# Low parts of weights all on VectorE, and GpSimd's convolution sums behind them, in a fused two-block transformer layer on one Trainium2 core

## The reference

```python
h = rms_norm(x, norm1_g[l])
z = h @ w_in[l].astype(h.dtype)
glu_in, q, k, v, gate_logits = jnp.split(z, SPLITS, axis=-1)
a_val, a_gate = jnp.split(glu_in, 2, axis=-1)
a = a_val * jax.nn.sigmoid(a_gate)
a = causal_depthwise_conv(a, conv_w[l], conv_b[l])      # 31 taps
a = jax.nn.silu(rms_norm(a, conv_norm_g[l]))
y_a = a @ w_conv_out[l].astype(a.dtype)
# q, k normed by head; attention in three dilated windows -> o
y_b = o @ w_attn_out[l].astype(o.dtype)
x = x + (g_a * y_a + g_b * y_b) @ w_out[l].astype(x.dtype)
```

## Time and profile before

| | before |
|---|---|
| median of 3 runs | 888.81 us |
| the profiled execution | 888.88 us, span 886.9 us |
| TensorE busy | 846.8 us, 95% |
| VectorE busy | 656.4 us, 74%, 1118 instructions |
| ScalarE busy | 555.2 us, 63% |
| GpSimd busy | 293.8 us, 33%, 292 instructions |
| low parts on VectorE (L1332) | 251, mean 1297 ns |
| low parts on GpSimd (L1863) | 16, mean 2592 ns |
| sums on GpSimd (L1912) | 90, mean 968 ns |
| granted TensorE clock, mean | 0.991 |

### The profile page before, as it was taken

How to read it: one execution, slowest core, us unless ns; L and a number is a source line. 1 busy time by engine, 2 the same in 40 slices (tenths; PEclk the granted TensorE clock), 3 DMA queues, 4 the chain that set the end, 5 groups by cost and what they waited for, 6 DMA issues and landing times.

```text
span 886.9 us, 16521 instructions
## 1 busy us (share of the span) xinstructions
PE 846.8 (95%) x5984; PEld 792.0 (89%) x5984; DVE 656.4 (74%) x1118; ACT 555.2 (63%) x1009; POOL 293.8 (33%) x292
## 2 busy tenths in 40 slices
PE   4999969999999999999999999999999999999996
PEld 3998969999998899999888988999997888888885
DVE  5988898897688889777676758747578866666552
ACT  5676976887655677666455675556645765555441
POOL 3799973445523234333121210001022332222111
PEclk9999999999999999999999999999999999999998
DMA  5564454444465547566565435335445466565641
GB/s 204 197 206 176 159 161 125 144 143 142 145 176 181 167 125 218 182 189 182 180 215 190 162 110 177 119 120 166 120 143 160 149 205 188 193 189 176 215 141 48
DMA packets 42304, 146.11 MB, mean 165 GB/s; under 512 B 4704, under 2 KB 7024, under 8 KB 42224
## 3 DMA queue, kind: packets, MB, share of 16 engines
q1 hardware_dynamic: 41472, 143.67, 50.8%
q10 hardware_dynamic: 752, 1.39, 0.4%
HBM read 144.00 MB, written 1.05 MB: 164 GB/s over the span
## 4 chain that ended last, share of the span: by engine, by line
PE 82%; DVE 8%; ACT 3%; issue 3%; POOL 1%; DMA 1%; DVEq 0%; ACTq 0%; POOLq 0%
PE px L516 20%; PE px L520 14%; PE px L522 14%; PE px L521 14%; PE px L517 10%; DVE wlo L1332 2%; PE px L562 2%; PE px L526 1%; PE px L528 1%; PE px L527 1%; DVE px L1391 1%; PE px L584 1%; PE px L719 1%; DVE sq L1347 1%; DVE hx L1353 1%
## 5 line engine op out<-in xcount | busy, mean ns | idle before, releaser
L1332 DVE TENSOR_TENSOR wlo<-raw,whi 128x1024 fp32r<-128x1024 f32 x251 | 323.9, 1297 | 32.9 <-ACT whi L858 32.7
L520 PE MATMUL px<-hx,whi 128*128 128x256 f32 x1072 | 312.3, 291 | 8.2 <-DVE hx L1353 5.0
L858 ACT ACTIVATE whi<-raw 128x1024 fp32r<-128x1024 f32 x267 | 279.9, 1052 | 57.3 <-PE px L517 28.0
L521 PE MATMUL px<-hx,whi 128*128 128x256 f32 x1072 | 304.6, 284 | 0.0
L522 PE MATMUL px<-hx,wlo 128*128 128x256 f32 x1072 | 304.5, 284 | 0.0
L520 PEld LDWEIGHTS px<-hx,whi 128*128 128x128 f32 x1072 | 206.8, 193 | 13.1 <-DVE hx L1353 6.1
L521 PEld LDWEIGHTS px<-hx,whi 128*128 128x128 f32 x1072 | 207.1, 193 | 0.4
L522 PEld LDWEIGHTS px<-hx,wlo 128*128 128x128 f32 x1072 | 206.8, 193 | 0.0
L516 PE MATMUL px<-fx,whi 128*128 128x512 f32 x330 | 115.7, 393 | 0.0
L516 PE MATMUL px<-hx,whi 128*128 128x512 f32 x320 | 111.3, 392 | 1.1 <-DVE hx L1353 1.1
L1912 POOL TENSOR_TENSOR CA<-CA,ct 128x256 f32<-128x256 f32 x90 | 87.1, 968 | 64.3 <-ACT ct L925 55.7
(11 more groups left out here) (300 smaller groups left out, 1363.5 us busy)
## 6 DMA issues: line engine op xcount, KB each, us to landing
raw<-ws SPq DMA_DIRECT2D x267, 512.0 KB, 3.7
tb<-tabs SPq DMA_DIRECT2D x16, 128.0 KB, 2.6
out<-X SPq DMA_DIRECT2D x4, 256.0 KB, 2.5
X<-xs SPq DMA_DIRECT2D x1, 512.0 KB, 4.7
X<-xs ACTq DMA_DIRECT2D x1, 512.0 KB, 4.8
vc<-vecs ACTq DMA_DIRECT2D x1, 320.0 KB, 6.6
msk<-lmask ACTq DMA_DIRECT2D x1, 256.0 KB, 2.9
ug<-pos ACTq DMA_DIRECT2D x1, 128.0 KB, 3.9
```

The costliest lines, as they stand in the source:

```text
L520: e.matmul(b[:, 0:S], H, xh, start=first, stop=False)
L521: e.matmul(b[:, 0:S], H, xl, start=False, stop=False)
L858: e.activation(whi[:, n % NSL, :], raw[:, n % NRAW, :], ACT.Copy).then_inc(s_hi, 1)
L1332: e.tensor_tensor(wlo[:, n % NSL, :], raw[:, n % NRAW, :], whi[:, n % NSL, :], ALU.subtract).then_inc(s_lov, 1)
```

## The change

All 267 low parts are now VectorE's; GpSimd's sixteen are gone, with their semaphore. GpSimd's sums of a chunk wait, up to chunk 56, until VectorE has made the low part that belongs to that step (`LOW[ahead(c)]`). The quotas of taps are new: VectorE 2.9 up to chunk 23, 2.6 up to 33, then 3.5; ScalarE/GpSimd 2.0 up to 33, then 1.8. The last taps now stand at chunk 52 instead of 55. Nothing of the computation changes.

```diff
@@ conv_plan
     for c in range(CONV_END + 1):
-        quota = (2.9, 2.0 if c < 24 else 1.7)
+        quota = (2.9 if c < 24 else 2.6 if c < 34 else 3.5, 2.0 if c < 34 else 1.8)
@@ semaphores
-        def on_gpsimd(c):
-            return c < 64 and c % 4 == 3
-
-        LOW = {}
-        for c in range(n_chunks):
-            n = c // 4 if c < 64 else 16
-            LOW[c] = (s_log, c // 4 + 1) if on_gpsimd(c) else (s_lov, c + 1 - n)
+        LOW = {c: (s_lo, c + 1) for c in range(n_chunks)}
@@ VectorE, lows
                     made[0] += 1
-                    if on_gpsimd(n):
-                        continue
                     e.wait_ge(s_hi, n + 1)
@@ GpSimd (lows and beside are removed, and every call of them)
             def taps(c):
+                if c in TAPS_G and c <= CONV_END:
+                    e.wait_ge(*LOW[ahead(c)])
                 for i, j in TAPS_G.get(c, ()):
@@ GpSimd, the loop over q, k and gate jobs
                 w, i = QKG[m]
-                beside((w, i))
                 taps(first_chunk((w, i)))
                 conv_square(first_chunk((w, i)))
```

More of the change, by code:

```diff
@@ L388, in two_blocks @@
         s_tb = [sem(f"s_tb{i}") for i in range(3)]
-        s_hi, s_lov, s_log, s_mm = sem("s_hi"), sem("s_lov"), sem("s_log"), sem("s_mm")
+        s_hi, s_lo, s_mm = sem("s_hi"), sem("s_lo"), sem("s_mm")
         s_bank = [sem(f"s_bank{i}") for i in range(8)]
@@ L1332, in lows @@
                     e.tensor_tensor(wlo[:, n % NSL, :], raw[:, n % NRAW, :], whi[:, n % NSL, :], ALU.subtract).then_inc(
-                        s_lov, 1)
+                        s_lo, 1)
             def beside(key):
@@ L1850, in _ @@
         def _(e):
[L1851 to L1868, removed]
             def low_tiles(inst, to, behind=None):
@@ L1923, in _ @@
                 for key in (("ag", i), ("av", i)):
-                    beside(key)
                     taps(first_chunk(key))
@@ L1928, in _ @@
                 for c in range(first_chunk(("v", n)), last_chunk(("v", n)) + 1):
-                    lows(ahead(c))
                     taps(c)
@@ L1940, in _ @@
                 qkg(m)
-            beside(("ao", 0))
             taps(CONV_END)
@@ L1947, in _ @@
             for i in range(1, KD):
-                beside(("ao", i))
                 for n in SILUS.get(i, ()):
```

## The result

The changed kernel takes 881.20 us (median of 5 runs, 881.03 to 883.95) against 888.81 us (887.64 to 890.41): a ratio of 0.9916, with an interval of 0.9896 to 0.9936. The forecast was 879.3 us and its range 877.0 to 885.5. The profiled execution took 881.09 us, for a span of 879.3.

What follows compares the result with a forecast made beforehand. TensorE's queue was taken to set the end, its one large wait being 7.3 us at the second scores for a late VectorE. Gains 8.1 - 0.6 + 0.6 + 1.5 = 9.6 us; 888.9 - 9.6 = 879.3 us, range 877.0 to 885.5.

Steps and rivals of the forecast that it cites:

- the forecast's own branch: The main outcome: a stop of 0 to 2.0 us at the second scores, 877.5 to 881 us, chance 0.74.
- one wait is several times all the others: TensorE's waits: 7.3 us once at the scores for VectorE, against 1.5 before w_conv_out and 0.6 at the start.
- start, GpSimd's low part of chunk 3: TensorE's small wait at the start: VectorE, idle there, can make this low part first; gain 0.6 us (0 to 0.6).
- second scores, stop and clock: At the second scores, VectorE frees TensorE's PSUM bank earlier: 9.05 less a remaining stop of 0.9, gain 8.1 us.
- attention steps: From 140 to 220 us: VectorE's load same or lower, but eight taps in chunks 38 and 39; 0.6 us lost.
- wait before w_conv_out: TensorE's 1.5 us stop for the last gated halves on VectorE goes; gain 1.5 us (0 to 1.5).
- I let it start there again: VectorE's stretch before the first softmax was assumed to start at 91.89 us as before, chunk 27's low part filling idle time.
- (a): Rival: blocked time partly moves, 0.62 us per step; 4.0 us stop at second scores, half clock, 884.1 us; chance 0.13.
- A low part rarely meets a sum any more: Before the first softmax, the added wait largely keeps GpSimd's sums off VectorE's low parts; 3.7 us blocked by sums taken.
- VectorE gets 1.14 for it and loses 2.7: Before w_conv_out: VectorE takes over one low part (1.14 us), and its gating falls from 3.81 to 1.1 us.
- (b): Rival: no relief, VectorE's 11.6 us of blocked time stay and only the small gains remain; 888.9 us; chance 0.05.
- (c): Rival: slower, the added wait releases both GpSimd sums against VectorE, 1.48 us blocked per step; 899 us; chance 0.08.

## Why the prediction was right, and the step that was not

The mechanism held. GpSimd's low parts blocked VectorE's K, Q and low parts; without them the first softmax comes early enough for TensorE to stop for 2 us instead of 7, and the clock stays up behind that stop. But the forecast's own branch was missed by a little: its range was 877.5 to 881 and its stop 0 to 2.0 us, against 881.2 and 2.13. Of its signs, the clock of 1.00 up to 250 us and the absence of a wait near 27 us came; low parts at 1.2 us did not (1.55), and four were missed narrowly: Q and K under 0.9 us (1.02), the softmax by 127 (127.48), scores less than 2.1 us behind the head sums (2.13), under 0.5 us before w_conv_out (0.52). Also, "one wait is several times all the others" holds only among the waits that the change can touch. The longest wait of TensorE is at the start, before and after:

```profile
PE px L541 <- DVE sqa L1369: 9.6, 1, 9.6
```

```profile
PE px L535 <- DVE sqa L1361: 9.9, 1, 9.9
```

Term by term, as gains:

| term | predicted | measured |
|---|---|---|
| start, GpSimd's low part of chunk 3 | 0.6 | 0.69 |
| second scores, stop and clock | 8.1 | 6.83 |
| attention steps | -0.6 | -0.58 |
| wait before w_conv_out | 1.5 | 0.97 |
| behind w_conv_out | 0 | -0.3 |
| sum, in the span | 9.6 | 7.6 |

**The start.** Right in place and size: 0.69 us by the head sums, and 1.00 in the second profile of the changed kernel, by the first scores (118.76 before, 117.76). Moving the tiles of chunks 3 and 63 alone removed it too.

**The second scores: the mis-sized term.** I took a stop of 0.9 us; it is 2.13. VectorE ended the softmax at 127.48 instead of the 127.0 forecast, and TensorE was there for the bank at 125.49 instead of 126.1, since the 0.69 us from the start had brought it forward. I had added the start's gain to the sum, though ahead of a stop that VectorE ends it only makes the stop longer. So to the third scores I had promised 8.7 us in all, and 7.52 came; of the 2.0 us by which the sum is too high, 1.2 lie here, 0.5 before w_conv_out and 0.3 behind it.

The end at 127.0 was nearly right by luck: two errors cancel. "I let it start there again" was wrong: the low part of chunk 28, which had started at 91.89, starts at 89.60, 2.3 us earlier, because ScalarE no longer waits for GpSimd's sums. I had read the releaser of that idle time (ScalarE's high part) and not what held ScalarE. And the blocked time is not 3.7 us. From 89.60 to 127.48 are 37.9 us; less 31.4 of own work and 0.3 of waiting, 6.2 us are blocked. By steps from 91.89 on, 3.4 of it falls on ten low parts (14.8 us for 10 x 1.14) and 2.4 on Q and K. That is 0.56 us per step, nearer to the 0.62 of rival (a) than to the 0.34 that I took. "A low part rarely meets a sum any more" fell: that was to be the work of the added wait, and the kernel without the wait has the same low parts (1525 and 1554 ns).

**The added wait.** I had put its cost at nothing, and no cost shows; but no gain shows either, and I had let it save part of the blocked time. What is saved goes by who comes first at chunk 24's step.

**The quotas.** I booked them as two taps less and as 0.6 us lost at the sixth scores. The second is what the runs show (a stop of 1.03 us there, of which 0.3 us are won back by the eleventh; with VectorE's quota old there is none). What I never priced is GpSimd's part, a quota of 2.0 for 1.7 from chunk 24 on. It makes the 2.13 us stop: without it there is none at the second scores. Its price is 3.3 us at w_conv_out between the variants with VectorE's quota old (241.03 against 237.76), of which some 1.5 is that profile's half clock.

**Before w_conv_out.** "VectorE gets 1.14 for it and loses 2.7" is what happened (the gating at L1458 takes 1.08 us for three instructions at 235.02), but TensorE still waits 0.52 us. I took the upper end of 0 to 1.5; measured 0.97.

**The rivals.** (a), 884.1, had the mechanism of the error right, blocked time that partly moves: 6.2 us. It needed 6.8 from 91.89 on, and a half clock, which came in three variants with nearly the same stop and not in this kernel. (b) is out. (c) needed 0.9 us blocked per step; over eleven steps there are 0.56. The rule that spoke against the change (the Trainium skill, Perfetto Trace Analysis, section Optimizing Scalar/DVE Operations: a saturated VectorE may hand work to GpSimd, unless the shared port spoils it) is settled by the run with the low parts alone: with the 16 tiles on GpSimd w_conv_out comes 11.6 us later. Its second half is the one that holds here.

**What stays open.** That the order of arrival at one step decides the next thirty microseconds is shown for its trigger, by one profile of one variant (one sum less in the step of chunk 24); what it is worth in time is not clear of the spread. How the state keeps itself up was read from the two groups of means, not tested: VectorE and GpSimd both take their pace from ScalarE's high parts and products, so an offset between them could persist. Why stops of 2.0 to 2.3 us brought a half clock in three of the kernels and none in the others was not settled. Nor was it settled why the part behind w_conv_out takes 635.1 us in one profile and 639.3 in another that has the same half clock.

## What to carry to other kernels

An instruction's duration in a profile may be mostly someone else's: look for the same form at its shortest, and for what the other engine runs beside its longest. When work moves between VectorE and GpSimd, price the blocked time on both, and follow what starts a stretch back more than one engine, since GpSimd's backlog came round through ScalarE as a late start on VectorE. And take a change with several parts apart: here one part was worth 11.6 us at w_conv_out and the parts added to help it gave 3.7 back.

## What the runs showed of the hardware

A VectorE instruction with two sources in SBUF and a GpSimd instruction that reads two tensors there hold each other up, in both directions. A Q of 0.48 us took 2.54 beside a GpSimd subtraction of 2.60, and GpSimd's sums went from 823 to 1218 ns where VectorE's low parts came first. VectorE's taps, with one source in PSUM, kept 0.48 us. Two memsets of 128 x 1024 (1.96 us) did not block the low part beside them. One small GpSimd instruction less, in one step, turned over which side loses for some 30 us (1554 to 1292 ns for the low parts, 823 to 1182 for the sums). The Trainium skill, SBUF — State Buffer, section Who interferes with whom, says that VectorE with two SBUF inputs contends with a GpSimd instruction that reads SBUF and not with one that only writes it, that the shared port is an exclusive lock, and that the order of issue decides who blocks. The runs agree with all three, by the numbers above.

The granted clock behind a stop is not a function of the stop's length alone. It was half for 3.4 us behind stops of 2.00, 2.09 and 2.32 us, and unchanged behind 2.01, 2.13 and 2.14 us. Each such half costs about 1.5 us (5.57 against 4.03 us between the second and third scores). Shorter stops can do it too, against what I took from the stop of 1.5 us at 249. Between 294 and 314 us every kernel has a stop of 0.7 and then one of 1.4 us. The changed kernel and the kernel before at that second stop, with the clock right behind it:

```profile
301.01 0.58 PE L514 MATMUL px<-hx,whi 128*128 128x256 f32 x1 [1.41 <-DVE hx L1345]
```

```profile
301.00:304.00 3.00, 2.98 (x14) 2.99 (x15) 2.29 (x5) 0.60 (x1) 0.55 (x1) 0.50 0.26 102
```

```profile
308.89 0.39 PE L520 MATMUL px<-hx,whi 128*128 128x256 f32 x1 [1.41 <-DVE hx L1353]
```

```profile
309.00:312.00 3.00, 3.00 (x24) 2.90 (x25) 2.29 (x6) 0.60 (x1) 0.43 (x1) 1.00 0.11 42
```

Of the 14 profiles 9 have the half clock at this place and 5 have not.
